# Gate and up weights of 27 experts in transfers of 2 MB with runs of 16 KB, in place of 1 MB halves with runs of 8 KB

## What is computed

```
def hier_moe(h, w_group, b_group, w_expert, b_expert, w_gate, w_up, w_down):
    ...
    gates = p_g[:, None] * jax.nn.softmax(top_v, axis=-1)
    expert_idx = (g_sel[:, None] * EXPERTS_PER_GROUP + top_j).astype(jnp.int32)
    ...
    def expert_block(args):
        x_b, e = args
        hid = jax.nn.silu(x_b @ w_gate[e]) * (x_b @ w_up[e])
        return hid @ w_down[e]
    ...
    return jnp.einsum('tkd,tk->td', y_assign, gates.astype(h.dtype))
```

## Time and profile before

| | |
|---|---|
| median of 3 runs | 938.07 us (938.05 to 938.66) |
| span of the profiled execution, first to last instruction | 936.1 us |
| median less that span, what lies around it | 1.97 us |
| TensorE busy | 858.2 us, 92% of the span |
| DMA, mean over the span | 284 GB/s |
| DMA in the experts' stage, 440 to 860 us | 400 GB/s |
| weights moved by SP's queue, whole span | 245.11 MB |

### The profile page before, as it was taken

How to read it: one execution, slowest core, us unless ns; L and a number is a source line. 1 busy time by engine, 2 the same in 40 slices (tenths; PEclk the granted TensorE clock), 3 DMA queues, 4 the chain that set the end, 5 groups by cost and what they waited for, 6 DMA issues and landing times.

```text
span 936.1 us, 16086 instructions
## 1 busy us (share of the span) xinstructions
PE 858.2 (92%) x5974; PEld 591.4 (63%) x5975; DVE 427.9 (46%) x641; ACT 248.6 (27%) x486; POOL 146.1 (16%) x287
## 2 busy tenths in 40 slices
PE   3989999999859999899998889998999999899984
PEld 2879978777638888865554445564555555565541
DVE  5399988866997433722222112222221222222256
ACT  5223174565575122011111111111111111111121
POOL 4200010000000110122221112222122222121203
PEclk9899999999989998999999999999999999999998
DMA  7443445221075456779999999999999999999984
GB/s 205 122 104 113 149 156 191 91 80 46 1 224 225 156 204 253 320 273 404 406 388 396 411 403 398 403 395 399 398 405 404 403 407 387 395 384 403 392 324 137
DMA packets 81932, 265.80 MB, mean 284 GB/s; under 512 B 19129, under 2 KB 44985, under 8 KB 57320
## 3 DMA queue, kind: packets, MB, share of 16 engines
q1 hardware_dynamic: 64272, 245.11, 68.8%
q0 software_dynamic: 7808, 18.56, 5.6%
q10 hardware_dynamic: 9816, 1.66, 1.0%
HBM read 247.53 MB, written 27.08 MB: 293 GB/s over the span
## 4 chain that ended last, share of the span: by engine, by line
PE 52%; DMA 24%; SPq 12%; DVE 7%; issue 2%; ACT 1%; ACTq 0%; POOL 0%; POOLq 0%; DVEq 0%
DMA big<-in_w_up 16%; PE ps L1027 13%; SPq L743 11%; PE ps L1255 8%; PE ps L1149 7%; PE ps L1292 5%; PE ps L1023 4%; DMA big<-in_w_down 3%; DMA ring<-in_w_up 3%; PE ps L1258 3%; DVE big L1644 2%; PE ps L1246 1%; PE ps L1169 1%; PE ps L1046 1%; PE ps L655 1%
## 5 line engine op out<-in xcount | busy, mean ns | idle before, releaser
L1258 PE MATMUL ps<-ring,big 128*64 128x256 f32 x704 | 159.0, 384 | 5.9 <-DMA ring<-in_w_up 5.8
L1255 PE MATMUL ps<-ring,big 128*64 128x256 f32 x704 | 159.3, 384 | 0.6 <-DMA ring<-in_w_gate 0.6
L1027 PE MATMUL ps<-hT,w_split 128*128 128x512 f32 (+1 forms) x768 | 146.0, 345 | 4.3 <-DVE hT L1600 3.8
L1919 DVE TENSOR_TENSOR big<-ps,big 64x256 f32<-64x256 f32 x78 | 33.2, 426 | 243.0 <-ACT big L1541 243.0
L1258 PE MATMUL ps<-big 128*64 128x256 f32 x544 | 122.0, 380 | 15.7 <-DMA big<-in_w_up 15.7
L1027 PEld LDWEIGHTS ps<-hT,w_split 128*128 128x128 f32 x768 | 118.6, 191 | 25.9 <-issue 11.4
L1255 PEld LDWEIGHTS ps<-ring,big 128*64 128x64 f32 x704 | 97.0, 139 | 54.8 <-issue 12.0
L1255 PE MATMUL ps<-big 128*64 128x256 f32 x544 | 122.8, 380 | 0.5 <-DMA big<-in_w_gate 0.5
L1644 DVE SCALAR_TENSOR_TENSOR big<-big,vec 128x783 f32<-128x783 f32 x116 | 119.6, 1031 | 3.0
L1258 PEld LDWEIGHTS ps<-ring,big 128*64 128x64 f32 x704 | 97.0, 139 | 14.6 <-DMA ring<-in_w_up 8.4
L1541 ACT ACTIVATE big<-ps 64x256 f32<-64x256 f32 x78 | 29.2, 375 | 265.5 <-PE ps L1258 265.5
(11 more groups left out here) (238 smaller groups left out, 1132.1 us busy)
## 6 DMA issues: line engine op xcount, KB each, us to landing
ring<-in_w_gate SPq DMA_DIRECT2D x44, 1024.0 KB, 29.0
ring<-in_w_up SPq DMA_DIRECT2D x44, 1024.0 KB, 29.7
ring<-in_w_down SPq DMA_DIRECT2D x44, 1024.0 KB, 30.0
big<-in_w_gate SPq DMA_DIRECT2D x20, 1024.0 KB, 30.1
big<-in_w_up SPq DMA_DIRECT2D x20, 1024.0 KB, 29.3
big<-in_w_down SPq DMA_DIRECT2D x20, 1024.0 KB, 30.2
w_raw<-in_w_in SPq DMA_DIRECT2D x20, 512.0 KB, 3.8
results<-spare POOLq DMA_DIRECT2D x12, 512.0 KB, 2.9
```

Of the source, the lines that this page charges most:

```text
L1027: mm = pe.matmul(ps[:, n % 2, 0:size], w_split[:, sub, hi_w, k, :], hT[:, k // 4, hi_h, k % 4, cols], **flags)
L1255: pe.matmul(ps[0:BLK, 6 * h, 0:FH], xT[:, k, :], gate_w[s][:, k, fs], start=(k == 0), stop=(k == KD - 1))
L1258: mm = pe.matmul(ps[BLK:2 * BLK, 6 * h + 1, 0:FH], xT[:, k, :], up_w[s][:, k, fs], start=(k == 0), stop=(k == KD - 1))
L1919: nc.vector.tensor_tensor(hb[:, fs], ps[BLK:2 * BLK, 6 * h + 1, 0:FH], sG[:, fs], ALU.mult).then_inc(hb_ready[h], 1)
```

## The change

The loop over places 3 to 29 waits for the whole gate-up of the slot's last block and then issues gate as one transfer of 2 MB and up as another, each with one run of 16 KB per partition. Down stays in two halves. The semaphores `gate_in` and `up_in` are now one for a slot, raised by 32 with such a transfer (and by 16 with each of the old pieces of places 0 to 2), and `gate_up` waits for both once, ahead of its first product. Places 30 and 31 keep the old pieces and waits (`load_last`, with semaphores `gate_end` and `up_end`; `target` is None for them).

```diff
-        gate_in = [[sem(f"gate_in{s}{q}") for q in range(2)] for s in range(SLOTS)]
-        up_in = [[sem(f"up_in{s}{q}") for q in range(2)] for s in range(SLOTS)]
+        gate_in, up_in = ([sem(f"{what}_in{s}") for s in range(SLOTS)] for what in ("gate", "up"))
+        gate_end, up_end = ([[sem(f"{what}_end{s}{q}") for q in range(2)] for s in range(E % SLOTS)] for what in ("gate", "up"))
...
-            def load_expert(i, s):
-                place = SLOTS * i + s
+            def expert_at(place):
                 e = sp.value_load(table[0:1, bass.ds(place + (3 * E + 2), 1)], min_val=0, max_val=E - 1)
                 end = sp.value_load(table[0:1, bass.ds(place + (2 * E - SLOTS), 1)], min_val=1, max_val=MAXB)
-                sp.wait_ge(gu_half, end)
-                load_some(e, s, 0, 2)
+                return e, end
+
+            def load_expert(i, s):
+                e, end = expert_at(SLOTS * i + s)
                 sp.wait_ge(gu_done[1], end)
-                load_some(e, s, 2, 4)
+                for to, w, landed in ((gate_w[s], w_gate, gate_in[s]), (up_w[s], w_up, up_in[s])):
+                    sp.dma_start(to, w[0, bass.ds(e, 1)].rearrange("e (p k) f -> p (e k) f", p=P)).then_inc(landed, 32)
+                sp.wait_ge(y_done, end)
+                load_some(e, s, 4, 6)
+
+            def load_last(place, s):
+                e, end = expert_at(place)
+                for q in range(2):
+                    ks = slice(q * KD // 2, (q + 1) * KD // 2)
+                    sp.wait_ge(gu_done[1] if q else gu_half, end)
+                    load(e, gate_end[s][q], gate_w[s], w_gate, ks)
+                    load(e, up_end[s][q], up_w[s], w_up, ks)
                 sp.wait_ge(y_done, end)
                 load_some(e, s, 4, 6)
...
             for place in range(E // SLOTS * SLOTS, E):
-                load_expert(place // SLOTS, place % SLOTS)
+                load_last(place, place % SLOTS)
...
                 for k in range(q * KD // 2, (q + 1) * KD // 2):
-                    if h == 0 and k % (KD // 2) == 0:
-                        pe.wait_ge(gate_in[s][q], target)
+                    if at_end and h == 0 and k % (KD // 2) == 0:
+                        pe.wait_ge(gate_end[s][q], 16)
+                        pe.wait_ge(up_end[s][q], 16)
+                    if not at_end and h == 0 and k == 0:
+                        pe.wait_ge(gate_in[s], target)
+                        pe.wait_ge(up_in[s], target)
                     pe.matmul(ps[0:BLK, 6 * h, 0:FH], xT[:, k, :], gate_w[s][:, k, fs], start=(k == 0), stop=(k == KD - 1))
-                    if h == 0 and k % (KD // 2) == 0:
-                        pe.wait_ge(up_in[s][q], target)
```

More of the change, by code:

```diff
@@ L732, in in_order @@
                     ks = slice(q * KD // 2, (q + 1) * KD // 2)
-                    yield gate_in[s][q], gate_w[s], w_gate, ks
-                    yield up_in[s][q], up_w[s], w_up, ks
+                    yield gate_in[s], gate_w[s], w_gate, ks
+                    yield up_in[s], up_w[s], w_up, ks
                 for q in range(2):
@@ L1249, in gate_up @@
             def gate_up(s, target, q, h):
+                at_end = target is None
                 fs = slice(h * FH, (h + 1) * FH)
                 for k in range(q * KD // 2, (q + 1) * KD // 2):
-                    if h == 0 and k % (KD // 2) == 0:
-                        pe.wait_ge(gate_in[s][q], target)
+                    if at_end and h == 0 and k % (KD // 2) == 0:
[4 more added lines that the diff above has]
+                        pe.wait_ge(up_in[s], target)
                     pe.matmul(ps[0:BLK, 6 * h, 0:FH], xT[:, k, :], gate_w[s][:, k, fs], start=(k == 0), stop=(k == KD - 1))
-                    if h == 0 and k % (KD // 2) == 0:
-                        pe.wait_ge(up_in[s][q], target)
                     mm = pe.matmul(ps[BLK:2 * BLK, 6 * h + 1, 0:FH], xT[:, k, :], up_w[s][:, k, fs],
@@ L1272, in turn_hidden, with expert_block @@
                 mm.then_inc(ht_ps[h], 1)
-            def expert_block(b, s, target):
+            def expert_block(b, s, target, down_target):
                 pe.wait_ge(xt_ready, b + 1)
@@ L1290, in expert_block @@
                         pe.wait_ge(ht_ready[k // (KF // 2)], b + 1)
-                        pe.wait_ge(dn_in[s][k // (KF // 2)], target)
+                        pe.wait_ge(dn_in[s][k // (KF // 2)], down_target)
                     pe.matmul(ps[0:BLK, 2, :], hbT[:, k, :], down_w[s][:, k, 0:512], start=(k == 0), stop=(k == KF - 1))
@@ L1300, in _, with expert @@
             stay_busy(3)
-            def expert(place, s, target):
+            def expert(place, s, target, down_target):
                 n = pe.value_load(table[0:1, bass.ds(place, 1)], min_val=1, max_val=MAXN)
@@ L1304, in expert @@
                 with pe.Fori(0, n) as j:
-                    expert_block(first + j, s, target)
+                    expert_block(first + j, s, target, down_target)
             with pe.Fori(0, E // SLOTS) as i:
                 for s in range(SLOTS):
-                    expert(SLOTS * i + s, s, 16 * i + 16)
+                    expert(SLOTS * i + s, s, 32 * i + 32, 16 * i + 16)
             for place in range(E // SLOTS * SLOTS, E):
-                expert(place, place % SLOTS, 16 * (place // SLOTS + 1))
+                expert(place, place % SLOTS, None, 16 * (place // SLOTS + 1))
             pe.wait_ge(late_ready, 1)
```

## The result

The changed kernel takes 952.07 us (948.13 to 954.05, 4 runs) against 938.37 us (938.05 to 943.86, 4 runs) for the kernel before beside it. The ratio is 1.0126, with a 95% interval of 1.0093 to 1.016. The prediction said 938.5, and at most 944.0. It was wrong: the change costs 1.3%.

The account below looks back on a forecast made before the run. TensorE was taken to follow the weights' transfers. At place 26, 3.43 + 3.40 - 5.2 = +1.6 us, less 1.25 at place 31, gave +0.4 and 938.5 us; the 8-in-10 range was 932.5 to 944.0.

Parts of the forecast that it names:

- late start: Place 3's first two transfers issue at 408.75 instead of 405.32, so every later weight landing comes 3.43 us later.
- wait for the whole: At place 26 TensorE starts its block only when all of up has landed, putting it 3.40 us later.
- longer runs: Fewer gate and up packets, at 13.5 ns each, save 0.216 us an expert, 5.2 us on weight landings by place 26.
- clock at place 26: Rival: TensorE's clock falls in place 26's single longer wait, adding 2.0 us, for 940.5 us; chance 0.10.
- wait at place 31: TensorE's last wait for weights, 1.25 us at 894.56, goes away.
- stage: The end of the experts' stage moves by +0.4 us, with the tail behind it unchanged.
- The first rival: Long runs save a third of the 16.8 us lost between queues, 5.4 by place 26: 933.1 us; chance 0.28.
- The sign that I had named: Weights alone at 430 GB/s would bear out the assumed price of a packet.
- The queue near 833: Thinnest place of the weights' queue: some 10 us of queued transfers remain after later issue and TensorE's lag.

Follow-up runs that it names:

- the turned kernel with 16 KB runs: The changed kernel with every second block's rows laid into the partitions in reversed order: 941.6 us (10 runs), ratio 1.0014.

## Why the prediction was wrong

| step | predicted | measured |
|---|---|---|
| late start, on the line | +3.43 | +3.52 alone (4.6 against an equal start); +3.31 and +4.31 with the one wait |
| wait for the whole | +3.40 | +3.45 at place 26; +3.43 in the stage when place 31 had it |
| longer runs, on the line | -5.2 | +4.4 and +5.0; +3.1 without the drift |
| clock at place 26 | 0 (rival: +2.0) | +1.75 in one execution, none in the other |
| wait at place 31 | -1.25 | gone, and worth -1.89 |
| stage | +0.4 | +11.9 and +11.1 |

**The step that failed is "the longer runs: -5.2 us on the weights' line by place 26".** It failed twice. The size of the own saving was half of what was taken: 6.7 ns a packet, 2.6 us. I had got 13.5 ns as a small difference of two large numbers from six microseconds with 42 long packets. Worse was the sentence "for a loss below zero I see no row: from 4 to 8 KB the rate rose". It made the trend of one step a bound for the next, and left out that each row is served beside the weights' packets and makes them last longer. The first rival saw that the two queues lose time to each other, 16.8 us in 440 to 860; I gave it the wrong sign. The loss isn't one for each change between queues, which would shrink with fewer packets; each row costs the engines more, 0.331 in place of 0.277 us, and the number of rows is the same. The sign that I had named, weights alone at 430 GB/s, didn't come either: they ran at 422 and 423.

**Late start and wait for the whole were right** in size, each alone and both together (+5.8 against 3.43 + 3.40 - 1.25 = 5.6). That the sum fits so closely is in part luck: the line was 0.9 us later than 3.43, and place 31 gave back 0.6 more than 1.25. The first issue of the loop stands at 409.89, 4.57 later than before, of which 1.16 is the later start of the stage: 3.41.

**Place 26.** Its up landed at 818.51, which on the line is 8.7 us later where I expected 1.8 earlier. The late start, the runs, the 3.40 and the clock (827.55 - 818.51 = 9.04 in place of 7.29 us) make 13.8 with the 0.9 that the kernel with the late issue and one wait has over 3.43. Place 31 gives back more than its 1.25 us of idle time. The last two turnings of rows of the kernel before, which have place 31's gate-up between them:

```profile
884.57 1.04 PE L1246 MATMUL ps<-ident,spare 64*128 64x64 f32 x8
...
898.45 1.05 PE L1246 MATMUL ps<-ident,spare 64*128 64x64 f32 x8
```

They are 13.88 us apart, and 11.99 in the changed kernel (899.51 to 911.50), where TensorE does not wait: 1.89 us. 13.8 - 1.9 = 11.9 is what the stage shows.

**The falls of the clock** were priced rightly (1.75 for 2.0) and judged too rare: six came, where I gave a chance of 0.10 to one at place 26. The waits of 3 us or more have their fall, in the kernels with the one wait and short runs as well; the late issue alone has neither. The one exception is a wait of 4.04 us in the turned kernel with 16 KB runs. The falls ahead of place 26 should be taken up by the next wait, as the rival said; TensorE does wait 3.10 us at place 26.

**The queue near 833** did run dry, where I expected some 10 us of cover: SP issued nothing from 816.3 to 851.51, and from 835 to 855 its queue used only 76.9% of the engines. DMA of the changed kernel there:

```profile
DMA packets 847, 6.60 MB, mean 330 GB/s; under 512 B 137, under 2 KB 137, under 8 KB 363
...
q1 hardware_dynamic: 546, 5.68, 76.9%
```

The 10 us counted on a few us of lag of TensorE at place 26, and it was 13.8. It cost nothing, since it lies behind the landing of place 26, and TensorE did not wait for places 30 and 31 at all.

## What to carry to other kernels

Where two queues share the DMA engines, price a change of run length by what the two queues' packets do to each other too, and measure it with and without the other queue; a gain from 4 to 8 KB promises none from 8 to 16. Loads that are waited for in halves hide half of a product and keep TensorE's gaps short (at most 1.9 us here, with none to two falls of its clock; with the one wait up to 5.2 us and five or six falls); one big transfer gives up both. And when indirect transfers move partly filled blocks, look at how far apart the engines finish: turning every second block over gave 0.6 to 0.9% here, while another deal of the rows made it worse.

## What the runs showed of the hardware

- A row of 4 KB on GpSimd's queue cost 0.277 us of engine time beside packets of 8 KB and 0.331 beside packets of 16 KB, though its own packet lasted 0.19 us beside either; the rest stands in the weights' packets. Why is open. The Trainium skill (DMA: Bandwidth & Descriptors, "Queues, rings and completion order") has each engine go round robin between its queues, a packet at a time. Turns alone, each packet whole, would leave a row's price as it is (an argument, not a measurement), and no run here shows what the engine does in the added 0.05 us.
- The 16 engines don't stay together over transfers of equal shares. They finished one transfer 15 to 16 us apart after 400 us of stage, 2 us apart when the rows were left out, and 4 to 6 us when every second block was turned over.
- With transfers of 1 MB to 64 neighbouring partitions the core moved 213 GB/s in place of 396, with transfers of 1 MB to every second partition 398.
- In the kernels with the one wait TensorE's clock fell to 1.2 GHz at all but one of the waits of 3 to 5 us and at 6 of 13 of those of 2 to 3 us, in a stage in which TensorE was otherwise busy. Products then took 0.63 us for 0.38, over 3 to 6 us. A wait of 1.67 us had a fall as well, while most as short had none.
